# Zero products on TensorE at six waits of a two-block transformer kernel

## The reference

```python
# first block
mixed = _mixer(_modulate(ctx, sh1c, sc1c), _modulate(x, sh1, sc1), ...)
x = _layernorm(ALPHA * x + g1 * (mixed[:, CTX_LEN:] @ w_out[l]), ln1_g[l], ln1_b[l])
ffn = _hier_moe(_modulate(x, sh2, sc2), ...)
x = _layernorm(ALPHA * x + g2 * ffn, ln2_g[l], ln2_b[l])
# second block
for i in range(DEPTH_2):                     # 2 layers
    h = rms_norm(x, norm_mix[i]) * (1.0 + sc1) + sh1
    y = mla_mixer(h, ...) if i % N_MIXERS == 0 else gdn_mixer(h, ...)
    x = x + g1 * y
    h = rms_norm(x, norm_ffn[i]) * (1.0 + sc2) + sh2
    y = swiglu_ffn(h, ...) if i % 2 == 0 else moe_ffn(h, ...)
    x = x + g2 * y
return rms_norm(x, final_norm)

def moe_ffn(h, w_router, w_gate_up, w_down):
    ...
    for e in range(N_EXPERTS_2):             # 8 experts, the best 2 per token
        y_e = swiglu_ffn(t, w_gate_up[e], w_down[e])
        out = out + combine[:, e:e + 1] * y_e
```

## Time and profile before

| | |
|---|---|
| time, median of 3 runs | 2305.46 us (2303.93 to 2309.15) |
| profiled execution, span from first to last instruction | 2302.1 us |
| PE busy (matmuls) | 2104.5 us, 91% of the span |
| PE weight loads busy | 1457.2 us, 63% |
| DVE / ACT / POOL busy | 793.3 / 427.9 / 38.1 us |
| mean granted clock of TensorE | 0.942 |
| chain that ended last | PE 83%, DVE 7%, ACT 4%, DMA 3%, issue 2% |
| DMA | 511.95 MB, 222 GB/s over the span |

### The profile page before, as it was taken

The page is one execution under the profiler, slowest core; times in us unless marked ns, Lnnn a source line. Parts: engine busy times, 40 slices in busy tenths (PEclk is TensorE's granted clock), DMA queues, the critical chain, the costliest instruction groups (busy, mean ns, idle before and its releaser), DMA issues.

```text
span 2302.1 us, 31821 instructions
## 1 busy us (share of the span) xinstructions
PE 2104.5 (91%) x13702; PEld 1457.2 (63%) x13702; DVE 793.3 (34%) x1639; ACT 427.9 (19%) x892; POOL 38.1 (2%) x34
## 2 busy tenths in 40 slices
PE   6999886887899999999899899999898889999998
PEld 4554664677744444444575678887777778648844
DVE  3494488555411111111234345424674320001001
ACT  2200243221311111111233310003322110000001
POOL 1000200000000000000000000000000000000000
PEclk9999896688999999999998999999998889999999
DMA  9610004204579999999744278753300077899696
GB/s 311 244 37 1 1 1 148 74 2 161 198 323 426 427 422 428 427 428 425 271 153 175 73 274 324 275 214 110 111 1 2 1 276 273 312 394 345 247 345 239
DMA packets 161862, 511.95 MB, mean 222 GB/s; under 512 B 9022, under 2 KB 32269, under 8 KB 149069
## 3 DMA queue, kind: packets, MB, share of 16 engines
q1 hardware_dynamic: 146352, 480.51, 54.2%
q10 hardware_dynamic: 15389, 29.67, 3.5%
HBM read 509.11 MB, written 1.05 MB: 222 GB/s over the span
## 4 chain that ended last, share of the span: by engine, by line
PE 83%; DVE 7%; ACT 4%; DMA 3%; issue 2%; SPq 0%; POOL 0%; ACTq 0%; DVEq 0%; POOLq 0%
PE PS L388 35%; PE PS L2406 10%; PE PS L2427 5%; PE PS L2560 4%; PE PS L2321 4%; PE PS L2332 4%; PE PS L2245 3%; DMA work<-in_moe_w_gate_up_dram 2%; PE PS L2511 2%; PE PS L857 1%; PE PS L629 1%; PE PS L849 1%; PE PS L637 1%; PE PS L1668 1%; DMA work<-in_w_ada_dram 1%
## 5 line engine op out<-in xcount | busy, mean ns | idle before, releaser
L388 PE MATMUL PS<-hT,work 128*128 128x256 f32 x1456 | 329.0, 386 | 4.5 <-ACT hT L919 4.0
L388 PEld LDWEIGHTS PS<-hT,work 128*128 128x128 f32 x1456 | 278.4, 193 | 50.7 <-issue 10.1
L388 PE MATMUL PS<-work 128*128 128x256 f32 (+4 forms) x960 | 284.0, 457 | 2.4 <-DVE work L1976 1.5
L388 PEld LDWEIGHTS PS<-work 128*128 128x128 f32 (+2 forms) x960 | 178.6, 187 | 105.8 <-issue 78.3
L2406 PE MATMUL PS<-work,sq 128*64 128x512 f32 x1024 | 222.6, 592 | 1.3 <-ACT sq L2350 1.3
L388 PE MATMUL PS<-sq,work 128*128 128x128 f32 x1408 | 162.9, 280 | 11.7 <-DMA work<-in_moe_w_gate_up_dram 11.7
L388 PEld LDWEIGHTS PS<-sq,work 128*128 128x128 f32 x1408 | 162.5, 197 | 13.7 <-DMA work<-in_moe_w_gate_up_dram 12.7
L2406 PEld LDWEIGHTS PS<-work,sq 128*64 128x64 f32 x1024 | 76.0, 137 | 144.5 <-issue 144.5
L2427 PE MATMUL PS<-work 128*64 128x512 f32 x512 | 113.4, 595 | 12.0 <-ACT work L2444 12.0
L2560 PE MATMUL PS<-work 128*64 128x512 f32 (+1 forms) x352 | 114.4, 593 | 2.0 <-ACT work L2590 2.0
L2388 DVE COPY work<-PS 128x1024 f32<-128x1024 f32 x22 | 26.9, 1225 | 232.4 <-PE PS L2427 119.1
(11 more groups left out here) (584 smaller groups left out, 2304.9 us busy)
## 6 DMA issues: line engine op xcount, KB each, us to landing
work<-in_ex_gate_dram SPq DMA_DIRECT2D x32, 2048.0 KB, 12.3
work<-in_ex_up_dram SPq DMA_DIRECT2D x32, 2048.0 KB, 15.4
work<-in_ex_down_dram SPq DMA_DIRECT2D x32, 2048.0 KB, 11.0
work<-in_moe_w_gate_up_dram SPq DMA_DIRECT2D x32, 2048.0 KB, 10.6
work<-in_moe_w_down_dram SPq DMA_DIRECT2D x16, 2048.0 KB, 14.5
work<-in_ada_w_dram ACTq DMA_DIRECT2D x14, 2048.0 KB, 11.4
work<-in_moe_w_gate_up_dram SPq DMA_DIRECT2D x16, 1536.0 KB, 13.4
work<-in_ada_w_dram SPq DMA_DIRECT2D x10, 2048.0 KB, 11.6
```

Of the source, the lines that this page charges most:

```text
L388: ins = pe.matmul(outp, lhs, rhs, start=n == 0, stop=n == len(pairs) - 1, **kw)
```

## The change

A new helper issues `n` products of the zeros matrix (128x128) by 512 columns of constants into one PSUM bank. Nobody reads what they write, nobody waits for them, and they signal nothing. It is called at six places, 36 products in all: 10 in `rw_inverse_pe`, between its first wait and its second; 7 ahead of `headnorm_pe(1, 0, yr)`; 4 ahead of `ex_pe("ffn")`; 5 ahead of `gd_triangles_pe(0)`; 4 between `gd_output_pe(2)` and `gd_output_pe(3)`; 6 behind the first gather of `ex_ranked_pe`, ahead of the loop.

```diff
+    def stay_busy_pe(bank, n):
+
+        for _ in range(n):
+            pe.matmul(PS[:, bank, :], zeros, consts[:, 0:512], start=True, stop=True)
...
     def rw_inverse_pe():
         all_emptied(pe, "bonus")
+        stay_busy_pe(4, 10)
         pe.wait_ge(S["hn_std"], 3)
...
         with_tokens_pe(name)
+        stay_busy_pe(7, 6)
         with pe.Fori(0, N_EXP2 // PER_LOOP[name]) as i:
...
         pe.wait_ge(S["gd_read"], 2)
+        stay_busy_pe(0, 5)
         gd_triangles_pe(0)
...
         gd_output_pe(2)
+        stay_busy_pe(2, 4)
         gd_output_pe(3)
...
             rw_step_pe(i)
+        stay_busy_pe(7, 7)
         headnorm_pe(1, 0, yr)
...
         out_pe("mla_out", oT, 8)
+        stay_busy_pe(2, 4)
         ex_pe("ffn")
```

## The result

The changed kernel took 2315.73 us, the median of 22 runs (2307.76 to 2324.41), against 2308.21 (2303.34 to 2319.19) for the kernel before in the same session: a ratio of 1.0024, with a 95% interval of 1.0013 to 1.0034. It is slower by 0.13 to 0.34%, where the forecast was 8 us, 0.35%, faster; 2315.73 lies outside the range. (The two medians stand 7.5 us apart, 0.33%; the ratio with its interval puts it at 5.5 us, 3.0 to 7.8.) Runs of either kernel differ by some 16 us, so the three runs known beforehand (spread 5 us) had said little of the noise.

The account below looks back on a forecast made before the run. TensorE was taken to bound the kernel (83% of a 2302.1 us span), its clock halving behind waits. Gains 3.0 + 2.6 + 1.8 + 0.6 = 8.0 us gave span 2294.1, time 2297.5 us; range 2291.5 to 2303.5.

Parts of the forecast that it names:

- Feed-forward net, minus 3.0: Four products in the 4.03 us wait: gate products start at full clock, half of about 6.1 us at 0.50 saved.
- Second mixture, minus 2.6: Six products ahead of the first expert: its 352 matmuls take 39.30 us like the second's, not 41.93.
- rival (b): Weight stream takes back the second mixture's 2.6 at 2077.49, full 2.1 overrun at the delta rule: 2301.2 us; chance 0.18.
- End of the delta rule, minus 1.8: Four products between output transposes: the projection behind gains 2.8 us, less 1.0 for products overrunning their 3.69 us wait.
- Triangles, minus 0.6: Five products: first triangles go from 1.91 to 1.28 us, clock falls later, the projection tile behind stays slow.
- Headnorm, 0: Seven products: clock falls again before the projection, which stays slow; bounds minus 2.3 and plus 0.4 us.
- Inverses, 0: Ten products: faster first half only waits longer for DVE; a clock fall could add up to 2 us.
- 72 matmul records and their weight loads more lie in waits: Closing step of the sum, for all six places: the added records lie in waits; no time was added for them.
- (c): Zero products do not hold the clock; the inverses' ten overrun, 11 us more in all, 2316.5 us; chance 0.06.

Follow-up runs that it names:

- third: Kernel before with only the five products ahead of the triangles and the four between the delta-rule outputs: 2309.96 us, ratio 0.9998 to the kernel before.
- sixth: Changed kernel plus 7 tiny products (32 columns of zeros by 8 of constants) at the headnorm: 2310.94 us, ratio 0.9986 to the kernel before.
- eleventh: Changed kernel without its groups at the inverses (10) and headnorm (7): 2306.24 us, ratio 0.9991 to the kernel before.
- second: Kernel before with only the ten products in the inverses and the seven ahead of the headnorm: 2320.54 us, ratio 1.0051 to the kernel before.
- ninth: Kernel before with only 17 tiny products (32 columns of zeros by 8 of constants) at the inverses: 2322.94 us, ratio 1.0049 to the kernel before.

## Why the prediction was wrong

By its own steps:

- **Feed-forward net, minus 3.0: right.** 41.23 became 38.23 us; the stretch gave 3.0 and 2.2 between pairs of profiles.
- **Second mixture, minus 2.6: right in kind, somewhat too large.** 2.4 in one profile, 0.6 in the other. Of the six profiles with these six products four have 43.6 us here, with 1.0 to 2.0 us left of the wait, and two have 45.3, with 2.6 and 2.8 left and the clock at 0.50 behind. The stream of weights did not give it back (1912 to 2090: 177.9 and 178.0 before, 177.8 and 177.6 after; the wait at 2077.49 grew by 0.4 and 0.5 us only), so rival (b) did not come about.
- **End of the delta rule, minus 1.8: the gain right, the overrun mis-sized.** The projection gave 3.2 in both. The overrun, of which I took 1.0 out of 0 to 2.1, was 2.5 in one profile (6.25 us in a wait of 3.69) and nothing in the other (3.70 us). In the third, sixth and eleventh kernel the four took 5.9 to 6.2 us again, so in four profiles of five some 2.4 are lost and about 0.8 is left, not 1.8. Where it was nothing, the clock was at 1.00 from 1794.3 on; where it was 2.5, it was at 0.50 when the products began, and it had been at 0.50 in part of the chunks ahead too, as this row of the changed kernel's first profile shows:

```profile
1800.00:1806.00 6.00, 5.98 (x28) 5.58 (x28) 3.48 (x5) 1.23 (x2) 0.00 (x0) 0.50 0.00 0
```

- **Triangles, minus 0.6: right** (0.3 to 0.7 in the stretch; first triangles 1.31, the tile behind still slow at 5.33). In the third and the sixth kernel the clock did not fall in the remaining 2.49 us, and the stretch gave 1.9 or more. **Headnorm, 0: right** (9.43).
- **Inverses, 0: slightly wrong**, by its own bound. The second half ran partly at 0.50 behind the gap of 2.17 us (5.40 against 3.95 us) in the first profile, and the stretch is 0.3 to 1.5 longer.
- **"72 matmul records and their weight loads more lie in waits": this step failed.** Read as execution time it is true. It took instructions to be free where their execution is hidden, and never asked what they displace. The rows for that question were in the trace: the wait of 3.11 us for "issue" behind a loop, one of 2.0 us in the inverses' tail, and a row of instruction transfers on the page. I read "issue 2%" in the earlier trace rows as overhead of the engine. It cost 5.6 us at the end of the first mixture and 3.2 behind the triangles; no rival had it. The rival for slower, (c), had the wrong mechanism: it has the clock fall in spite of the zero products, and the clock rose. Its 2316.5 us lie beside the measured 2315.73 by luck.

The sum with the means of both pairs of profiles: gains 2.6 (feed-forward), 1.5 (expert), 2.0 (3.2 less half of 2.5), 0.5 (triangles), together 6.6 against my 8.0. Losses 5.6 and 3.2, the inverses 0.9, and 1.9 in 1810 to 1866 and behind 1912, together 11.6. That leaves 5.0 us slower, where the ratio says 5.5 (3.0 to 7.8). So close a match is partly luck: each term is a mean of two profiles that differ by up to 2.5 us. The stretches left out of this sum are those that differ within one kernel by as much as between the two. So the gain was not lost to another wait of the same kind: it arrived, and the two stretches in which the moved instruction stream stalls cost 8.8 us, more than all of it. **What is still open:** why the second transfer behind the loop starts only 5.9 to 6.0 us after the first, where elsewhere in before two start 3.1 us apart. The DMA engines are full of weights there (share 1.05 from 1129 to 1132 us of after), but the transfers themselves last 0.9 to 1.1 us, no longer than elsewhere (0.88 to 1.4 in before), and no run here changed the stream of weights. Open too are the clock behind the stall in the tiny burst, the waits for "issue" in the second mixture's experts, and the last microseconds of the second and ninth kernel.

The range was too narrow above: its width came from the terms of the sum, and one unknown, where everything behind 144 new instructions comes to stand, was left out.

## What to carry to other kernels

Idle time is not the only thing that an inserted instruction uses: it moves everything behind it against the borders of the instruction transfers, and a loop's exit or a burst of tiny instructions hundreds of microseconds later may start to stall. Before adding filler, read all waits for "issue" over half a microsecond, see which of them end just behind an instruction transfer, count the instructions to those, and afterwards compare the same waits first; a few fillers more or fewer can undo the loss, as seven more did here. Put filler only where long dense work follows (two places gave as much as four, within the intervals), and compare second profiles of each kernel before explaining a stretch.

## What the runs showed of the hardware

- Instructions of TensorE arrive in 16 KB transfers of 256 while the kernel runs. The exit of the first mixture's loop cost 2.4 to 3.3 us in eight profiles, and 6.8 to 7.1 us in the five in which 10 instructions of the current transfer were left (five records and five loads ran, then came the second stall). In all thirteen the second transfer starts 5.9 to 6.0 us after the first. That 64 products cost nothing and 17 cost 0.49% was not expected from any row.
- 256 matmuls of 16x16 run in 2.33 us and use two transfers; a border late in such a burst or at its end costs 1.8 to 2.5 us, one ten records into the dense matmuls behind it 0.21.
- Zero products hold the clock by their work, not by being there: with 128x512 the feed-forward products start at 1.00, with 32x8 in the same number they take 2.0 us longer. Behind four full ones (5.9 to 6.3 us, begun at 0.50) the clock was at 1.00 again, behind two (3.78 us) it was not.
- The same short wait can keep the clock or lose it. Behind the 1.95 us of the earlier trace rows (1.92 to 1.95 in all profiles) it fell to 0.50 in eleven profiles and stayed at 1.00 in two; behind the 2.1 to 2.2 us left in the inverses it fell in three and stayed in one; behind the 2.5 left ahead of the triangles it fell in four and stayed in two; a remaining 2.0 us (first expert) kept it at 1.00. The Trainium skill, "TensorE: Matmul & The Clock Gate", section "Why this matters for your kernels", advises against idle gaps over about three microseconds. In this kernel gaps well under that were followed by the low clock; whether other short waits nearby had a part in it, no run here separates.
- Not every wait for "issue" is an instruction transfer's: those of 2.3 us in the second mixture's experts end 29 us behind the last one in before.
